# Stick-breaking stage: the high and low parts of the next head pair's projection pieces made at other items

## What is computed

```python
h = rmsnorm(x, g_mix[i])
proj = h @ w_in[i]
p0, p1, p2 = jnp.split(proj[..., :3 * MIX_WIDTH], 3, axis=-1)   # q, k, v of 16 heads
# per block of queries:
z = jnp.einsum("bhqd,bhkd->bhqk", qb, kf) * scale
log_keep = jnp.where(mask, jax.nn.log_sigmoid(-z), 0.0)
later = lax.cumsum(log_keep, axis=3, reverse=True) - log_keep
log_a = jax.nn.log_sigmoid(z) + later
a = jnp.where(mask, jnp.exp(log_a), 0.0)
out = jnp.einsum("bhqk,bhkd->bhqd", a, vf)
```

## Time and profile before

| what | value |
| --- | --- |
| time, median of 3 runs | 2652.38 us |
| span of the profiled execution | 2646.9 us |
| PE busy in the span | 2562.6 us (97%) |
| DVE busy | 1784.0 us (67%) |
| ACT busy | 1204.7 us (46%) |
| POOL busy | 719.9 us (27%) |
| the stage with its eight pairs | about 1340 to 1890 us of the span |

### The profile page before, as it was taken

How to read it: one execution, slowest core, us unless ns; L and a number is a source line. 1 busy time by engine, 2 the same in 40 slices (tenths; PEclk the granted TensorE clock), 3 DMA queues, 4 the chain that set the end, 5 groups by cost and what they waited for, 6 DMA issues and landing times.

```text
span 2646.9 us, 34791 instructions
## 1 busy us (share of the span) xinstructions
PE 2562.6 (97%) x12320; PEld 2130.7 (80%) x12320; DVE 1784.0 (67%) x2247; ACT 1204.7 (46%) x2027; POOL 719.9 (27%) x523
## 2 busy tenths in 40 slices
PE   8899999999999999999999999998899999999999
PEld 8688887888888887887878888886788888887887
DVE  6566666167756577775677777777648665758667
ACT  6463333144434443335666666665424443444332
POOL 2502220102323222233033333333120322222322
PEclk9899999999999999999999999999999999999999
DMA  6412225213433456534111111112321342437634
GB/s 208 152 40 72 78 90 191 80 63 116 146 116 119 151 177 246 217 147 159 49 37 33 33 32 32 32 32 107 125 101 53 139 161 77 152 133 273 236 145 157
DMA packets 85923, 311.39 MB, mean 118 GB/s; under 512 B 10417, under 2 KB 10417, under 8 KB 73137
## 3 DMA queue, kind: packets, MB, share of 16 engines
q1 hardware_dynamic: 74304, 261.17, 28.0%
q0 software_dynamic: 11216, 42.47, 4.5%
q10 hardware_dynamic: 288, 6.29, 0.6%
HBM read 220.24 MB, written 89.65 MB: 117 GB/s over the span
## 4 chain that ended last, share of the span: by engine, by line
PE 79%; DVE 7%; issue 7%; ACT 4%; POOL 1%; DMA 1%; SPq 0%; ACTq 0%; DVEq 0%; POOLq 0%
PE ps L2334 25%; PE ps L2336 24%; PE ps L2335 24%; PE ps L2646 1%; POOL sig L968 1%; DVE aT_lo L1955 1%; PE ps L2662 1%; DVE tile_lo L2203 1%; DVE w_lo L1584 1%; DVE keep L1913 1%; ACT keep L1313 1%; PE ps L2663 1%; PE ps L2595 1%; ACT sq L1325 1%; PE ps L2596 1%
## 5 line engine op out<-in xcount | busy, mean ns | idle before, releaser
L2334 PE MATMUL ps<-tile_hi,g_hi 128*128 128x512 f32 x1680 | 661.3, 394 | 7.7 <-DVE tile_lo L2203 5.2
L2336 PE MATMUL ps<-tile_hi,g_lo 128*128 128x512 f32 x1680 | 658.3, 392 | 0.0
L2335 PE MATMUL ps<-tile_lo,g_hi 128*128 128x512 f32 x1680 | 654.7, 390 | 0.0
L2334 PE MATMUL ps<-xg_hi,w_hi 128*128 128x512 f32 x1024 | 412.6, 403 | 4.5 <-DVE xg_lo L1783 3.3
L2336 PE MATMUL ps<-xg_hi,w_lo 128*128 128x512 f32 x1024 | 402.6, 393 | 0.0
L2335 PE MATMUL ps<-xg_lo,w_hi 128*128 128x512 f32 x1024 | 402.1, 393 | 0.0
L2334 PEld LDWEIGHTS ps<-tile_hi,g_hi 128*128 128x128 f32 x1680 | 316.2, 188 | 76.1 <-issue 5.5
L2336 PEld LDWEIGHTS ps<-tile_hi,g_lo 128*128 128x128 f32 x1680 | 316.0, 188 | 71.5
L2335 PEld LDWEIGHTS ps<-tile_lo,g_hi 128*128 128x128 f32 x1680 | 316.3, 188 | 69.0
L1482 ACT ACTIVATE g_hi<-quads 128x512 fp32r<-128x512 f32 x310 | 194.9, 629 | 359.0 <-PE ps L2336 328.8
L2132 DVE TENSOR_TENSOR g_lo<-quads,g_hi 128x512 fp32r<-128x512 f32 x310 | 281.4, 908 | 107.1 <-ACT g_hi L1482 103.1
(11 more groups left out here) (277 smaller groups left out, 4338.4 us busy)
## 6 DMA issues: line engine op xcount, KB each, us to landing
quads<-wpack SPq DMA_DIRECT2D x62, 1024.0 KB, 5.9
raw<-wpack SPq DMA_DIRECT2D x88, 512.0 KB, 3.3
d_split<-x SPq DMA_DIRECT2D x116, 256.0 KB, 6.3
tile_lo<-d_tile SPq DMA_DIRECT2D x30, 512.0 KB, 7.5
d_tile<-R SPq DMA_DIRECT2D x46, 256.0 KB, 6.4
d_tile<-x SPq DMA_DIRECT2D x46, 256.0 KB, 6.1
cquads<-wpack SPq DMA_DIRECT2D x10, 1024.0 KB, 4.8
tile_hi<-d_split SPq DMA_DIRECT2D x10, 1024.0 KB, 8.5
```

Of the source, the lines that this page charges most:

```text
L2334: pe.matmul(out, whi, mhi, start=start, stop=False, skip_group_check=chained)
L2335: pe.matmul(out, whi, mlo, start=False, stop=False, skip_group_check=chained)
L2336: return pe.matmul(out, wlo, mhi, start=False, stop=stop, skip_group_check=chained)
```

## The change

Two tables say at which item a piece's high parts (SPLIT_HI, on ACT) and low parts (SPLIT_LO, on DVE) are made. Before, both were made at the same items: pieces 0 and 1 at the very end of items 1 and 2, behind o_low and o_sum, pieces 2 and 3 in items 4 and 5, ahead of them. Now:

- ACT: piece 0 in item 1, piece 1 in item 2, ahead of o_low instead of behind it; pieces 2 and 3 as before.
- DVE: piece 0 in item 2, behind chunk 2 and ahead of o_sum; piece 1 in item 3, ahead of chunk 2; piece 2 as before in item 4; piece 3 in item 6, behind chunk 2 and ahead of o_sum.

The lines of the changed kernel's functions lie 3 to 5 higher in number.

```diff
+        SPLIT_HI = {1: 0, 2: 1, 4: 2, 5: 3}
+        SPLIT_LO = {2: 0, 3: 1, 4: 2, 6: 3}
...
 # ACT, pair()
-                            if not last and it in (4, 5):
-                                project(hp + 1, 1 - par, it - 2)
+                            if not last and it in SPLIT_HI and t < 2:
+                                project(hp + 1, 1 - par, SPLIT_HI[it])
                             for c in range(2, t + 1):
                                 chunk(hp, it, c, first)
                                 if it == ITEMS - 1 and not last:
                                     project(hp + 1, 1 - par, 4 + c)
+                            if not last and it in SPLIT_HI and t >= 2:
+                                project(hp + 1, 1 - par, SPLIT_HI[it])
                             rows = slice(hh * SHEAD, (hh + 1) * SHEAD)
                             act.wait_ge(pv_done, hp * CHUNKS + CHUNKS_BEFORE[it + 1])
...
                             act.activation(o_low[rows, :], ps[SHEAD:P, 6, 0:2 * P], ACT.Copy
                                            ).then_inc(o_low_ready, 1)
-                            if not last and it in (1, 2):
-                                project(hp + 1, 1 - par, it - 1)
...
 # DVE, pair()
-                            if not last and it in (4, 5):
-                                lo_part(hp + 1, 1 - par, it - 2)
+                            if not last and it in SPLIT_LO and t != 2:
+                                lo_part(hp + 1, 1 - par, SPLIT_LO[it])
                             for c in range(2, t + 1):
                                 finished(c)
                                 chunk(hp, it, c)
...
                             if t >= 1:
                                 finished(t + 1)
+                            if not last and it in SPLIT_LO and t == 2:
+                                lo_part(hp + 1, 1 - par, SPLIT_LO[it])
...
                             dve.wait_ge(o_low_ready, hp * ITEMS + (it + 1))
                             dve.tensor_tensor(dst, ps[0:SHEAD, 6, 0:2 * P], o_low[rows, :], ALU.add
                                               ).then_inc(o_sum_ready, 1)
-                            if not last and it in (1, 2):
-                                lo_part(hp + 1, 1 - par, it - 1)
```

## The result

The changed kernel takes 2689.7 us (median of 4 runs, 2681.1 to 2690.1) where the kernel before takes 2652.0 us beside it (4 runs): a ratio of 1.0137, 95% interval 1.0124 to 1.0150. It is slower by 37.7 us. The prediction had the sign and most of the waits, but 2666.4 us and an upper end of 2675.

The account below looks back on a forecast made before the run. PE was taken as the bound, busy 63.66 of 66.76 us a pair. 2652.4 us plus 12.3 for seven pairs of 1.75 gave 2664.7, plus 1.7 for one clock fall 2666.4; range 2657.5 to 2675 us.

Parts of the forecast that it names:

- Part 1: Items 1 and 2: without piece 0's low parts, PE's chunk 2 comes 0.73 us earlier, gap 0.88 to 0.15.
- Part 2: Item 2, behind the scan: piece 0's first low part waits for POOL's product until 1430.85, both through at 1432.17.
- Part 3: Item 3: piece 1's low parts ahead of chunk 2 cancel a 0.73 us lead and lose 0.45; bounds 0, 0.9.
- Part 4: Piece 3's low parts at item 6's end delay item 7's first matmul, losing 1.3 us a pair; bounds 0.9, 1.5.
- the sum without the clock: Losses in items 3 and 7, 0.45 + 1.3 = 1.75 us a pair, 12.3 us in seven pairs.
- PE's clock: At the new 2.4 us gap before item 7: one fall counted, 1.7 us; ends no fall and seven falls, 12 us.
- the clock falls in most of the seven gaps: Rival at the new gaps before item 7: 2664.7 + 5 x 1.7 or more, 2673 to 2677 us; chance 0.15.

Follow-up runs that it names:

- short_product: The changed kernel, but in item 6 POOL multiplies only 128 columns of the 1024-column row: 2658.4 us, ratio 1.0026.
- lo3_back: The changed kernel with piece 3's low parts back in item 5 instead of item 6: 2658.4 us, ratio 1.0022.
- lo3_only: The kernel before with only piece 3's low parts moved, to item 6 behind chunk 2: 2668.7 us, ratio 1.0055.
- late_q_lo3: late_q with piece 3's low parts in item 6 behind chunk 2: 2663.1 us, ratio 1.0041.
- half_lo3: The changed kernel with one of piece 3's two low parts back in item 5, the other left in item 6: 2666.2 us, ratio 1.0062.
- late_q: The changed kernel, but DVE makes low parts of piece 0 ending item 3, piece 1 in item 4, piece 3 in item 5: 2640.4 us, again 2641.4.
- hi_only: ACT's order of the changed kernel with DVE's order of the kernel before: 2646.9 us, ratio 0.9979.
- run 63: Not a label but a verb and a count: the changed kernel with 9 useless matmuls before PE's sk_lo wait, 2675.9 us, ratio 1.0089.

## Why the prediction was right and wrong

**Part 1 (piece 0 leaves the junction): right.** PE's gap before chunk 2 of item 2 shrank to 0.16 us, the text had 0.15. In item 6 it shrank to 0.26, where the text's 0.8 us off the 0.88 left 0.1.

**Part 2 (a low part behind POOL's product): right.** 2.86 us for the pair, the text's times give 2.84. That POOL causes such a delay was then shown in item 6, by short_product; item 2 has the same form and was not tested by itself.

**Part 3 (item 3): the sign right, 0.73 us instead of 0.45.** The mis-sized term is POOL's 0.64 us product of the 256-column row. The text took it as costing the same wherever it fell, 0.5 us. It fell behind w_lo, at its full length ahead of the low part, which made that pair 2.10 us where an undisturbed one has 1.40: 0.7 us. That is 0.2 of the difference; the text's own terms, without rounding on the way, give 1437.84 for aT_lo and 0.51 us, which is the rest but for 0.02. lo3_back measures this part by itself, and 0.73 lies inside the bounds of 0 to 0.9.

**Part 4 (item 7): right.** A wait of 2.38 us, the text's 2.4, and 1.34 us lost where it had 1.3, measured by lo3_only and once more by late_q_lo3.

So the sum without the clock is 7 x (0.73 + 1.34) = 14.5 us and not 12.3.

**PE's clock: the step that failed.** The text said "I count one fall: 1.7 us", reasoning that dense work on both sides of the gap would protect it. The profiled execution has a fall in all seven pairs at 2.8 us each (71.72 − 68.90), 19.7 us. Both factors were too small. The count: dense work on both sides does not prevent the fall, as lo3_only (two falls), late_q_lo3 (six) and the changed kernel (seven) show with practically the same wait. The price: the text took 4 us at a clock of 0.57 from the last pair, while here the clock stayed at the lower level for 6.83 us, about 6 of them after the wait. The rival "the clock falls in most of the seven gaps" named the mechanism, but with the same price of 1.7 us it ended at 2677, and the range was cut below even that. Its own end of 12 us for seven falls stood in the text, and on top of 2664.7 would have given 2676.7 at most; with the measured price it gives 2684 and 2687 with part 3's true size.

**The rest of the profiled difference.** The span grew by 41.4 us, from 2646.9 to 2688.3. 14.5 + 19.7 are 34.2. In hp 0 the clock fell once more, behind the wait of 1.78 us in item 3, for 3.4 us (an estimate of its cost from half the clock: 1.7 us). The last pair, whose instructions are the same, took 82.96 us with a clock of 0.90 instead of 80.52 at 0.94, and the stage began 3.4 us later. The last two are not the change's: the runs of the kernel before differ among each other by up to 8 us, and the last pair takes 80.5 to 83.0 us in the profiled executions of all kernels here.

**What stays open.** Why the clock falls at some waits of 2.4 us and not at others of the same length. In the changed kernel it falls in every pair, with pairs of 71.7 us, in lo3_only in two, with pairs of 68.2 us. What the traces add is that the falls come evenly: in the changed kernel they begin 71.68 us apart, pair after pair, and in late_q_lo3 five of them 68.27 us apart, with pairs of 68.25. Where one began 0.38 to 1.01 us before the end of the sk_lo wait (nine falls, in three kernels) the clock stayed low for 6.8 us; where it began 0.15 to 0.19 us before the end (six falls, in two of them), or behind it (the one in half_lo3), it stayed low for 3.4. Pairs that are all equally long meet such a fall at about the same point each time, which fits that falls come in rows of pairs and that their price is alike; it was not tested by itself.

The faster versions show why the change's aim was sound. Taking q's low parts out of items 1 and 2 is worth what part 1 says, if they go where DVE waits for PE (late_q), and not to places ahead of something that PE needs. The pair of late_q is 1.4 us shorter than before, of which ACT's order alone gives 0.74 (hi_only).

## What to carry to other kernels

Before moving a DVE instruction with two SBUF operands into an idle stretch, look at what POOL does in that stretch, and at who waits for its result: an idle 1.26 us took in a pair of 1.40 that became 2.86. Where PE gets a new wait of some 2.4 us, price it twice: the wait, and the clock behind it, which here cost up to twice the wait's own loss (2.8 us against 1.34); carry a range up to a fall in every repetition of the loop, since it was two, six and seven of seven pairs here. A semaphore wait at the head of the next block (here sqk_lo_ready) is the due time of a moved step, and the step should land where its engine is waiting for the bounding engine anyway.

## What was not expected of the hardware

- A single wait of PE of 2.4 us in otherwise dense work can let the granted clock fall to the 1.2 GHz level (0.50), for 3.4 us at some waits and 6.8 at others. The waits of 1.66 to 1.72 us in hp 1 to 6 never did in the profiled executions, 36 of them in five kernels. In hp 0 the clock did fall, behind a wait of 1.78 to 1.80 us in item 3 in all five, and behind one of 1.54 us in half_lo3; whether length or place decides is open.
- Filling the wait with useless matmuls gave 14 us back, although it had PE run 63 matmuls more.
- The execution with these added matmuls had one wait of 4.6 us in PE's instruction stream at the start of a pair that no semaphore explains.
